# Modulation sums moved out of a projection stage, and that stage's slots put in another order

## What is computed

```python
h = layer_norm(DN_ALPHA * h + y, ln_g[l], ln_b[l])            # end of the first block
...
silu_c = jax.nn.silu(c)
silu_cc = jax.nn.silu(c_ctx)
for i in range(DEPTH_2):                                      # DEPTH_2 = 2
    shift, scale, gate = jnp.split((silu_c @ ada_w[i] + ada_b[i])[:, None, :], 3, axis=-1)
    a = modulate(rmsnorm(x, norm_g[i]), shift, scale)         # h * (1 + scale) + shift
    if ctx_out or m in (0, 2):
        shift_c, scale_c, gate_c = jnp.split(silu_cc @ ada_w[i] + ada_b[i], 3, axis=-1)
        ac = modulate(rmsnorm(xc, norm_g[i]), shift_c, scale_c)
    if m == 0:
        y, yc = mla_mixer(a, ac, cos, sin, mla_w_in[j], ...)  # cq, ckv, kr, gate; then q, k, v; 8 heads
    elif m == 1:
        y = hyena_seq(a, hy_w_in[j], ..., hyena_filter_spectra(L, *filt), hy_bias[j], hy_w_out[j])
    x = x + gate * y
return rmsnorm(x, final_g)
```

## Time and profile before

| | us |
|---|---|
| median of 3 runs | 3030.62 |
| lowest and highest | 3029.76, 3033.29 |
| the profiled execution | 3030.52 |
| its span in the trace | 3028.7 |
| PE busy in it | 2740.2 (90%) |
| DVE busy | 1878.6 (62%) |
| ACT busy, POOL busy | 894.8 (30%), 810.6 (27%) |

### The profile page before, as it was taken

The page is one execution under the profiler, slowest core; times in us unless marked ns, Lnnn a source line. Parts: engine busy times, 40 slices in busy tenths (PEclk is TensorE's granted clock), DMA queues, the critical chain, the costliest instruction groups (busy, mean ns, idle before and its releaser), DMA issues. The chain is left out here.

```text
span 3028.7 us, 30579 instructions
## 1 busy us (share of the span) xinstructions
PE 2740.2 (90%) x11377; PEld 1868.9 (62%) x11377; DVE 1878.6 (62%) x2979; ACT 894.8 (30%) x1519; POOL 810.6 (27%) x486
## 2 busy tenths in 40 slices
PE   7999989978689978788999999996999998999967
PEld 3544434547456556566778899995778885444456
DVE  6256239999576668755851555554785533888564
ACT  2111121100344332435434565552332211111122
POOL 0000000004021135565432233324542220343234
PEclk9999999989889989899999999997999999999979
DMA  4211411110100034143856323214421123111043
GB/s 151 81 70 63 142 62 42 35 43 1 56 1 1 1 146 160 63 142 127 280 188 206 93 57 91 68 38 134 144 84 49 42 70 149 59 59 59 28 167 111
DMA packets 109560, 269.78 MB, mean 89 GB/s; under 512 B 18464, under 2 KB 34664, under 8 KB 105001
## 3 DMA queue, kind: packets, MB, share of 16 engines
q1 hardware_dynamic: 109418, 267.90, 26.5%
HBM read 206.87 MB, written 60.99 MB: 88 GB/s over the span
## 5 line engine op out<-in xcount | busy, mean ns | idle before, releaser
L313 PE MATMUL psum<-part,part 128*128 128x512 f32 (+1 forms) x1984 | 766.9, 387 | 94.4 <-POOL part L1598 49.2
L314 PE MATMUL psum<-part,part 128*128 128x512 f32 (+1 forms) x1984 | 744.4, 375 | 0.0
L315 PE MATMUL psum<-part,part 128*128 128x512 f32 (+1 forms) x1984 | 742.9, 374 | 0.0
L1598 POOL TENSOR_TENSOR part<-arena,part 128x1024 fp32r<-128x1024 f32 (+1 forms) x149 | 370.8, 2489 | 712.3 <-ACT part L1592 712.3
L313 PEld LDWEIGHTS psum<-part,part 128*128 128x128 f32 x1984 | 379.8, 191 | 183.4 <-POOL part L1598 95.5
L314 PEld LDWEIGHTS psum<-part,part 128*128 128x128 f32 x1984 | 380.4, 192 | 71.3 <-issue 3.2
L315 PEld LDWEIGHTS psum<-part,part 128*128 128x128 f32 x1984 | 379.2, 191 | 71.6
L221 PE MATMUL psum<-arena 128*128 128x512 f32 (+1 forms) x672 | 232.4, 505 | 17.3 <-DMA arena<-in_w_f 10.0
L1592 ACT ACTIVATE part<-arena 128x1024 fp32r<-128x1024 f32 (+1 forms) x149 | 155.4, 1043 | 262.9 <-PE psum L315 183.0
L1135 POOL TENSOR_TENSOR arena<-arena 128x256 f32<-128x256 f32 x56 | 38.2, 682 | 705.2 <-PE psum L1148 705.2
L2413 DVE TENSOR_REDUCE arena<-psum 128x1 f32<-128x1280 f32 x64 | 95.5, 1492 | 175.9 <-PE psum L2365 175.9
(11 more groups left out here) (311 smaller groups left out, 4074.4 us busy)
## 6 DMA issues: line engine op xcount, KB each, us to landing
arena<-in_ada_w SPq DMA_DIRECT2D x24, 1024.0 KB, 5.3
arena<-in_w_hy SPq DMA_DIRECT2D x40, 512.0 KB, 3.2
scratch_spec<-arena SPq DMA_DIRECT2D x68, 256.0 KB, 2.0
arena<-scratch_spec SPq DMA_DIRECT2D x12, 1024.0 KB, 5.3
arena<-in_w_gate SPq DMA_DIRECT2D x16, 512.0 KB, 4.1
arena<-in_w_out SPq DMA_DIRECT2D x16, 512.0 KB, 4.0
arena<-in_w_mgate SPq DMA_DIRECT2D x16, 512.0 KB, 4.1
arena<-in_w_mout SPq DMA_DIRECT2D x16, 512.0 KB, 3.5
```

What stands on the lines that cost most here:

```text
L313: nc.tensor.matmul(acc, a_hi, b_hi, start=start, stop=False)
L314: nc.tensor.matmul(acc, a_hi, b_lo, start=False, stop=False)
L315: return nc.tensor.matmul(acc, a_lo, b_hi, start=False, stop=stop)
L1598: self.K.nc.gpsimd.tensor_tensor(self.lo[s][:, 0:n], self.raw[s][:, 0:n], self.hi[s][:, 0:n].bitcast(F32), ALU.subtract).then_inc(self.spl ...
```

## The change

1. **Sums with both conditions.** The 16 tiles with two dot products each leave the gates stage. They now stand in the first stage: two tiles (four dot products of 128x1024, and two loads of 512 KB) behind `take_latent(t)` of each of the token tiles 1 to 8. Buffers for them are made by computing the decay in two halves: eight exps of 128x512 ahead, and sixteen of 128x256 later, between the evacuations of the spectra; the order in which the filters' products are made follows it. The condition's row is stored to a scratch tensor.
2. **The other 32 sums** go to the second attention: one dot product behind the last subtraction of iteration i, for i from 4 to 50 unless 3 divides i (tile n = 0, 1, 2, ...). SP loads two tiles ahead of DVE, tile by tile, with two buffers; in its program these loads stand behind the gate tile of a head and ahead of the wait for the next head's inverses. The biases are added in iteration 52.
3. **The slot in the gates stage.** ACT and DVE evacuate first; ACT's round comes right behind it; on POOL the rest is first. The norm steps stand behind, with new tables.

The core of the diff:

```diff
@@ class AdaSums (now above stage_spectra_tokens)
+    def load(self, sp, i):
+        if i < len(self.order):
+            if i >= 2:
+                sp.wait_ge(self.used, i - 1)
+            sp.dma_start(self.w[i % 2], self.K.dram["ada_w"][:, self.order[i], :]).then_inc(self.loaded[i % 2], 16)
...
@@ stage_spectra_tokens
                 sp.dma_start(dram["vN"][0:n, t, :], vN_slot[t % 3][0:n, :]).then_inc(v_out[t % 3], 16)
+                if t:
+                    for i in range(2 * t - 2, 2 * t):
+                        A.load(sp, i + 2)
...
                         for t in range(1, 9):
                             take_latent(t)
+                            for i in range(2 * t - 2, 2 * t):
+                                A.work(dve, i)
                         norm_latents()
...
             for t in range(TT):
-                ins = nc.scalar.activation(decay[:, t, :], delta, ACT.Exp, scale=K.col("neg_t", t))
+                ins = nc.scalar.activation(decay[:, 0, t, :], delta, ACT.Exp, scale=K.col("neg_t", t))
             ins.then_inc(decay_ready, 1)
+            A.silu(act)
...
+                if 5 <= n < 13:
...
+                    for q in range(2):
+                        ins = nc.scalar.activation(decay[:, 1, n - 5, 256 * q:256 * q + 256], delta_late[q], ACT.Exp,
+                                                   scale=K.col("neg_t", n - 5))
...
@@ stage_gates_to_keys
-    CHAIN = {0: dict(center=18, sums1=20, stats1=21, scale={21: [0, 1], 22: [2, 3, 4], 23: [5, 6, 7]}, sums2=25, stats2=26,
...
+                     square1={18: [0, 1], 19: [2, 3], 20: [4, 5], 21: [6, 7]}, sums1=22, stats1=23,
...
+                     square2={25: [0, 1, 2], 26: [3, 4, 5], 27: [6, 7]}, sums2=28, stats2=29,
...
-    X_ADD = {12: [1, 2, 3], 13: [4], 14: [5], 15: [6], 16: [7], **{25 + k: [8 + k] for k in range(1, 8)}}
...
+    X_ADD = {8 + 16 * j + k: [8 * j + k] for j in range(2) for k in range(1, 8)}
...
-                if 49 <= u <= 64:
-                    A2.load(sp, u - 49 + 2)
...
             W.rest(pool, 0)
             W.rest(pool, 1)
             for u in range(NU):
+                if users[tile_of[u]] == u + 1 and tile_of[u] + 2 < NW:
+                    W.rest(pool, tile_of[u] + 2)
                 if 2 <= u < 10:
                     NC.add(pool, u - 2)
...
-                if users[tile_of[u]] == u + 1 and tile_of[u] + 2 < NW:
-                    W.rest(pool, tile_of[u] + 2)
             mla.gpsimd(pool)
...
@@ mla_attention
+    ADA_AT = {i: 2 * (i // 3) + i % 3 - 3 for i in range(4, 51) if i % 3}
...
+        def load_modulation(n):
+            if n < 32:
+                if n >= 2:
+                    sp.wait_ge(ada_used, n - 1)
+                sp.dma_start(ada_w[n % 2], dram["ada_w"][:, 16 + n, :]).then_inc(ada_in[n % 2], 16)
...
             sp.dma_start(gate[h % 2], dram["gate"][:, h, :]).then_inc(gate_in, 16)
+            for i in range(8 * h, 8 * h + 8):
+                if i in ADA_AT:
+                    load_modulation(ADA_AT[i] + 2)
             sp.wait_ge(inverted, h + 1)
...
+                if i in ADA_AT:
+                    n = ADA_AT[i]
...
+                    dve.wait_ge(ada_in[n % 2], 16 * (n // 2 + 1))
+                    v.tensor_tensor_reduce(ada_w[n % 2], ada_w[n % 2], condition, 1.0, 0.0, ALU.mult, ALU.add,
+                                           K.ada[:, 16 + n, 0:1]).then_inc(ada_used, 1)
```

More of the change, by code:

```diff
@@ L484, in stage_spectra_tokens @@
     latents_out = K.sem("latents_stored")
+    A = AdaSums(K, list(range(16)), 16, (7168, 8192), 5120, K.view(45568, D))
+    condition_out = K.sem("condition_stored")
     def h_tile(k, t):
@@ L568, in make_weights @@
             def make_weights():
[L569 removed]
+                dve.wait_ge(loads, 16 * 6)
                 v.tensor_tensor(w_ed[0:64, :, 0, :], w_fb[0:64, :, 0, :], w_fb[0:64, :, 1, :], ALU.add)
@@ L1616, in __init__ @@
         self.acc = K.view(acc, max(widths))
-        self.sums = [K.bank(b, n) for b, n in zip(banks, widths)]
+        self.banks, self.sums = banks, [K.bank(b, n) for b, n in zip(banks, widths)]
         self.rstd = [K.view(at, n) for at, n in zip(rstd, widths)]
@@ L2098, in _ @@
                     W.round(act, tile_of[u] + 2)
+                if u == 2:
+                    act.wait_ge(ctx_in, 16)
+                if 2 <= u < 10:
+                    NC.square(act, u - 2)
+                if u == 11:
+                    NC.root(act, 0)
+                if u in (28, 29):
+                    for k in range(4 * (u - 28), 4 * (u - 27)):
+                        act.wait_ge(ctx_scaled, k + 1)
+                        a(ctx_hi(k), ctx[:, k, :], ACT.Identity, bias=K.ada[:, SHIFT + k, 1:2]).then_inc(ctx_rounded, 1)
@@ new lines, in _ @@
+                if u + 2 in QSTAT:
+                    for k in range(3):
+                        NQ.square(act, 3 * QSTAT[u + 2] + k)
+                if u in QSTAT:
+                    NQ.root(act, QSTAT[u])
+                for n in QAPPLY.get(u, []):
+                    jj, k = ORDER_Q[n]
+                    act.wait_ge(q_applied, n + 1)
+                    a(cq_hi[:, k, cols(jj)], cq[:, k, cols(jj)], ACT.Copy).then_inc(q_rounded, 1)
+                if u + 2 in KSTAT:
+                    for k in range(2):
+                        NK.square(act, 2 * KSTAT[u + 2] + k)
@@ L2099, in _ @@
+                if u in KSTAT:
+                    NK.root(act, KSTAT[u])
+                for n in KAPPLY.get(u, []):
+                    jj, k = ORDER_K[n]
+                    act.wait_ge(k_applied, n + 1)
+                    a(ckv_hi[:, k, cols(jj)], ckv[:, k, cols(jj)], ACT.Copy).then_inc(k_rounded, 1)
             mla.scalar(act)
@@ L2238, in _ @@
                         v.tensor_tensor(dst, dst, tmp, ALU.add).then_inc(roped, 1)
+                if u == 11:
+                    NC.mean(dve, 0)
+                    NC.invert(dve, 0)
+                if u in (12, 13):
+                    for k in range(4 * (u - 12), 4 * (u - 11)):
+                        v.scalar_tensor_tensor(out=ctx[:, k, :], in0=ctx[:, k, :], scalar=K.modA[:, 1, k:k + 1],
+                                               in1=stat[:, 0:CTX], op0=ALU.mult, op1=ALU.mult).then_inc(ctx_scaled, 1)
```

404 lines of the change are left out of this document (179 added, 225 removed).

## The result

| | us |
|---|---|
| changed kernel, median of 8 runs | 3043.78 (3039.35 to 3059.25) |
| kernel before, median of the 8 runs beside it | 3032.66 (3029.76 to 3034.67) |
| ratio | 1.0043, 95% interval 1.0028 to 1.0059 |
| profiled execution and its span | 3046.56, 3044.8 |

A forecast was written before the change was run, and what follows sets the result against it. PE bounds the kernel: stalls lose 90.5 us in the gates stage, and the second attention has no slack. 3030.5 - 5.5 (first stage) - 37.5 (gates stage) + 52.6 (second attention) = 3040 us, range 3008 to 3062.

The forecast's parts named there:

- The two halves of the decay: First stage: decay's first half ready earlier, filter products 5.7 us shorter, token tile 1 gives back 2.6; -8.3 us.
- The turning of the latents: First stage: the last portion of dot products, ahead of the latents' norm, delays PE's turning; +2.8 us.
- The sum of what is left: Gates stage, slots 0 to 64: 54.0 of 90.5 us of losses remain, so 36.5 gained.
- Slots 28 and 29: Gates stage: POOL's rests and adds from slot 25 on run late against PE; 10.2 us still lost.
- slots 32 to 35: Gates stage, within slots 29 to 35: half-length slots and heavy DVE work, waits for sums, splits and weights; 14 us lost.
- slots 46 and 49: Gates stage, within slots 45 to 49: late squares' sums, and ACT waiting before evacuating slot 47; 10.8 us lost.
- the lock of the earlier trace: Gates stage: DVE and POOL each wait for the other's whole instruction; dot products took up to 3.47 against 1.21 us.
- the rest first in the slot: Gates stage: POOL's rest costs PE nothing where evacuation, round and rest, 4.2 us, fit into a 5.57 us slot.
- The sum of the stalls: Second attention: DVE waits for late weights in five heads, four of 9.3 to 10.1 us, one 3.3; 41.6 us.
- the time from the store of the inverses to SP's next issue: Second attention, end of a head: SP gets on when the store has landed, 1720.29 to 1729.04 at head 1.
- Rival A: Second attention: weights come early enough, each stall some 3 us, that part +23, kernel 3010.5 us; chance 0.15.
- The clock: Second attention: PE's granted clock falls behind the five stalls, costing 11 us (7 to 20) on top.

The follow-up runs named there:

- e9_best: Changed kernel, ones-matmuls one slot later, attention products re-placed, weights issued before SP's store wait, last two first-stage tiles' products behind the latents' norm: 2961.77 us.
- e3_old_stage: Changed kernel with each head's first modulation tile issued before SP's store wait, and the earlier kernel's gates stage without modulation sums: 3014.16 us, ratio 0.9950.
- e6_weights_last: Changed kernel with first weights issued before SP's store wait and ones-matmuls one slot later, but ACT's round and POOL's rest last in each slot: 3021.44 us.
- e1_early: Changed kernel with each head's first modulation tile issued between the store of the inverses and SP's wait for it: 3011.57 us, ratio 0.9939.
- e2_noloads: Changed kernel with 30 of the second attention's modulation loads left out, all 32 dot products reading the first tile: 2991.05 us, one run.

## Why the prediction came out as it did

It forecast 3040 us, slower by some 10, and 3043.78 was measured, slower by 11.1. In the traces the three stages are off by 1.7, 1.4 and 6.6 us, and the two stretches that were put at nothing by 1.5 and 4.5. Step by step:

**First stage.** The two halves of the decay gave what was worked out: PE began the spectra 8.3 us earlier (122.62 and 114.32), which is -8.3 to the tenth. (The filter products end at 43.98 instead of 49.99, 6.0 earlier, and the token tile behind them gave back 2.3, where 5.7 and 2.6 had been given.) The turning of the latents was put at +2.8 and cost 1.1:

```profile
114.32 5.39 PE L840 MATMUL psum<-arena 128*128 128x512 f32 x12 [0.73 <-issue]
119.64 2.34 PE L797 MATMUL psum<-arena 16*128 16x16 f32 x9
```

The nine turns take 2.34 us, where the earlier trace rows has 1.25. The step that was mis-sized is the lead of PE: I took the end of the nine norms as what PE waits for, but it can begin with the first. In e9_best, where the last products stand behind the norms, the nine take 1.25 again, and this 1.1 comes back.

**Gates stage.** The sum of what is left was forecast at 54.0 and is 52.9, but that agreement hides misses that cancel. Slots 28 and 29 lost 9.3 (10.2 forecast), slots 32 to 35 10.4 (14), slots 46 and 49 14.0 (10.8). Slot 23, with its sum of slot 22, lost 6.2 where the same sum and slot 40's had been given 3.1 together: POOL's adds in slots 18 to 21 took 1.5 to 1.7 us each beside DVE's centering, and were late by a slot. I had the lock of the earlier trace rows in hand and applied it only to slots 25 to 27. And the text left open which half of the change gives the gain; it is the absence of the sums, 31 of 39 us (e3_old_stage). Its one sentence on how they cost PE time, through POOL and the lock, missed the loads: in slots 4 to 13 SP's wait for DVE held back the stage's own weights. The size came out right because the working counts what is left and not what goes. Meanwhile the point that the prediction held for the order, the rest first in the slot, is worth 33 us, together with ACT's round, only once the sums are late (e6_weights_last). That PE's wait at a sum is one of place and not of work, and could be taken away by moving it, the prediction did not see.

**Second attention.** The mechanism is as predicted: waits in five heads, at iterations 11, 19, 28, 35 and 43, the third the short one, released by in_ada_w, and e1_early takes most of them away by moving one issue of each head, e9_best all of them, with the products' places moved too. The sum of the stalls was mis-sized: 41.6 forecast, 48.8 measured. The term that failed is the time from the store of the inverses to SP's next issue, 8.75 us for the first head by the earlier trace rows and read in the same way for the others. Over the five heads whose end brings a wait it was 46.4 us in the kernel before and 52.8 in the changed one (11.2 at the first): 6.5 of the 7.2 us. The weights landed one tile's time behind the gate tile, as said: the gate tile landed 11.6 us after 1688.34, at 1699.9, and the dot product began at 1701.2, 9.6 us after the issue of its tile at 1691.58.

```profile
arena<-in_ada_w SPq DMA_DIRECT2D x2, 512.0 KB, 10.0
...
arena<-scratch_gate SPq DMA_DIRECT2D x1, 512.0 KB, 11.6
```

Rival A, the weights that overtake the queue, did not come: they came in the order of issue. The rule of the Trainium skill that spoke for it ("DMA: Bandwidth & Descriptors", section "Queues, rings and completion order") says only that this order is not guaranteed, which no run here contradicts. The clock cost 9.2 (430.9 less the 372.9 of e9_best, less 48.8), 11 forecast. That POOL could hold a product was priced at nothing; e2_noloads shows four such places and one in iteration 4. In the changed kernel the four lie in iterations that wait for weights anyway.

**The rest.** +4.5 us after the attention were not forecast; they are told of below.

So the forecast was right by its mechanisms in the first stage and in the attention. In the gates stage it was closer than its working deserves, and that the whole came within 4 us is in part luck: the errors by stage go in both directions (-3.1 us in the first stage and the gates stage, +6.6 in the attention), and the two profiled executions lie 5 us further apart than the medians.

## What to carry to other kernels

Before a load is put behind others in one issuing engine's program, ask what that engine waits for there: here a wait for an unrelated store, which was never on the critical path, became part of the latency of each head's first weights, and issuing them ahead of that wait cost nothing. The kernel before had the same trap the other way round, modulation loads with a wait of their own ahead of the stage's weights. The lists of waits name the DMA or POOL's rest and never SP's own wait: one has to follow the late load back to its issue. Where the slots of the other engines begin with the evacuation of the unit just made, a small matmul that feeds a later step of that same slot need not stand a slot earlier; it only gives the engine that adds for it less time. And when two halves of a change pull in opposite directions, read stage by stage: 0.4% slower was 39 us won and 59 lost, and both could be improved on.

## What the runs showed of the hardware that was not expected

After the attention the program is the same in all kernels here, and yet it took 4.5 us longer in the changed one, 3.5 of them in the stage of the long convolutions. PE's waits there are equal (14.2 and 14.3 us for DVE, in four waits), but the clock behind them is not. Ten us from the end of the wait of 3.6 us and of that of 2.3 us, in the kernel before

```profile
2740.79:2750.79 10.00, 10.00 (x20) 4.35 (x21) 6.04 (x10) 0.00 (x0) 9.54 (x8) 0.83 0.49 147
2820.54:2830.54 10.00, 10.00 (x24) 4.50 (x25) 7.76 (x13) 0.00 (x0) 7.97 (x8) 1.00 0.56 208
```

and in the changed one

```profile
2754.17:2764.17 10.00, 10.00 (x17) 4.38 (x18) 5.01 (x9) 0.00 (x0) 9.53 (x8) 0.72 0.48 145
2834.96:2844.96 10.00, 10.00 (x20) 4.50 (x21) 6.14 (x11) 0.00 (x0) 7.63 (x7) 0.84 0.60 209
```

The same wait of 2.3 us left the clock at 1.00 in one execution and at 0.84 in the other. All eight profiles of kernels with the change have a long-convolution stage 3 us or so longer than the one profile of the kernel before. Whether that is due to anything in the change, or to how the waits fall against whatever the clock goes by, no run here decides; it stays open. It is also a warning for reading such tables: 3 to 4 us of clock can move in code that nobody touched.
